# Layer input's gate in three fp32r products, the router's products inside mix_out, output weights in eight pieces, last units scaled by VectorE

## What is computed

```python
x = _layer_norm(DEEPNORM_ALPHA * x + m @ w_out, ln1_g, ln1_b)
# _moe: the router
scores = jax.nn.sigmoid((x @ w_router).astype(f32))        # 16 experts in 4 groups
biased = scores + router_bias
gsel   = argmax over groups of the sum of the two best
eidx   = the two best experts in that group
dest   = place of each (token, expert) pair in rows padded to 128 per expert
# layer input
ple_term = (ple @ w_ple) * jax.nn.sigmoid(x @ w_ple_gate)  # ple: 256 columns
x = _layer_norm(DEEPNORM_ALPHA * x + ffn + ple_term, ln2_g, ln2_b)
```

## Time and profile before

| | us |
|---|---|
| time before, median of 3 runs (2895.13 to 2896.97) | 2895.21 |
| the profiled execution | 2897.11 |
| its span, first to last instruction | 2895.0 |
| mix_out's first transfer to route's first | 2004.1 to 2157.7 |
| route's first transfer to the experts' first | 2157.7 to 2371.3 |
| experts' first transfer to the end | 2371.3 to 2895.0 |

### The profile page before, as it was taken

One profiled execution on the slowest core, in us unless ns is written; L12 is line 12 of the kernel. 1 busy time (PEld: TensorE's weight loads), 2 busy tenths in 40 slices (PEclk: granted clock), 3 DMA queues, 4 the chain that ended last, 5 costly groups with the idle time before them and its releaser, 6 DMA issues. The chain is left out here.

```text
span 2895.0 us, 41255 instructions
## 1 busy us (share of the span) xinstructions
PE 2533.8 (88%) x16099; PEld 2013.9 (70%) x16099; DVE 1236.3 (43%) x2155; ACT 1019.4 (35%) x1412; POOL 693.4 (24%) x537
## 2 busy tenths in 40 slices
PE   8989699969978996788868999997989979999991
PEld 7966456659958994777747888885447427877770
DVE  1042366645426654444431111110432107888876
ACT  1100277752232224455411111110001127777763
POOL 2231145432224324443301111110001430001002
PEclk9989699989989997999856999998987989999995
DMA  4363700021100004000040111112130029999986
GB/s 134 81 178 92 204 1 2 1 91 51 36 11 1 1 1 159 30 31 23 30 167 33 44 43 43 43 36 87 37 126 30 0 87 362 398 390 387 395 315 262
DMA packets 86455, 321.76 MB, mean 111 GB/s; under 512 B 14670, under 2 KB 35934, under 8 KB 66134
## 3 DMA queue, kind: packets, MB, share of 16 engines
q1 hardware_dynamic: 64966, 266.20, 25.4%
q10 hardware_dynamic: 12752, 28.14, 2.9%
q0 software_dynamic: 8608, 25.65, 2.5%
HBM read 281.40 MB, written 42.74 MB: 112 GB/s over the span
## 5 line engine op out<-in xcount | busy, mean ns | idle before, releaser
L2687 DVE TENSOR_TENSOR ex_low<-ex_raw,ex_high 128x2048 fp32r<-128x2048 f32 x138 | 308.7, 2287 | 141.3 <-ACT ex_high L2683 140.6
L2683 ACT ACTIVATE ex_high<-ex_raw 128x2048 fp32r<-128x2048 f32 x138 | 256.3, 1910 | 25.9 <-ACT o L2877 15.3
L172 PE MATMUL ps<-hx_high,mg_wg 128*128 128x344 f32 x576 | 191.6, 333 | 6.9 <-POOL mg_wg L2260 6.9
L174 PE MATMUL ps<-hx_low,mg_wg 128*128 128x344 f32 x576 | 185.1, 321 | 0.0
L173 PE MATMUL ps<-hx_high,mg_wg 128*128 128x344 f32 x576 | 184.8, 321 | 0.0
L1035 POOL TENSOR_SCALAR np_z<-np_z,np_sm 128x640 f32<-128x640 f32 (+12 forms) x128 | 125.4, 1003 | 231.1 <-DVE np_sm L1001 231.1
L2278 PE MATMUL ps<-o,hx_wb 128*128 128x344 f32 x576 | 170.4, 452 | 0.0
L2260 POOL TENSOR_TENSOR mg_wg<-hx_raw,mg_wg 128x1024 fp32r<-128x1024 f32 x24 | 56.4, 2352 | 429.4 <-ACT mg_wg L2288 429.4
L2698 PE MATMUL ps<-ex_high,ex_xh 128*128 128x512 f32 x368 | 150.3, 408 | 8.3 <-DVE ex_xl L2921 8.3
L2699 PE MATMUL ps<-ex_high,ex_xl 128*128 128x512 f32 x368 | 146.9, 399 | 0.0
L2700 PE MATMUL ps<-ex_low,ex_xh 128*128 128x512 f32 x368 | 146.6, 398 | 0.0
(11 more groups left out here) (556 smaller groups left out, 5967.7 us busy)
## 6 DMA issues: line engine op xcount, KB each, us to landing
ex_raw<-in_w_eg SPq DMA_DIRECT2D x46, 1024.0 KB, 7.2
ex_raw<-in_w_eu SPq DMA_DIRECT2D x46, 1024.0 KB, 9.4
ex_raw<-in_w_ed SPq DMA_DIRECT2D x46, 1024.0 KB, 9.8
hx_raw<-in_w_mg SPq DMA_DIRECT2D x24, 512.0 KB, 3.9
scratch_s_rows<-o ACTq DMA_DIRECT2D x23, 512.0 KB, 8.5
dnp_w<-in_w_dn SPq DMA_DIRECT2D x16, 512.0 KB, 3.4
hg_raw<-in_w_hg SPq DMA_DIRECT2D x16, 512.0 KB, 3.5
ns_pg<-in_cache SPq DMA_DIRECT2D x32, 192.0 KB, 2.8
```

The source lines that it names most:

```text
L172: pe.matmul(out, w[:, 0, k, :], x.high[:, k, tokens], start=first, stop=False)
L174: return pe.matmul(out, w[:, 0, k, :], x.low[:, k, tokens], start=False, stop=final)
L2683: act.activation(self.high[:, q], self.raw[:, q], ACT.Copy).then_inc(self.high_done[q], 1)
L2687: eng.tensor_tensor(self.low[:, q], self.raw[:, q], self.high[:, q], ALU.subtract).then_inc(self.low_done[q], 1)
```

## The change

- **mix_out**: w comes in eight transfers, one per contraction step, each with its own semaphore; the first half of tile 0's products waits for each in turn. The router's weights rw are loaded here. TensorE makes the router's products of tile t-2 after the products of tile t (the last two behind them), from an fp32 copy xf of one transposed tile, into PSUM bank 6. ScalarE copies a transposed tile twice: rounded to x1.high and exactly to xf. VectorE subtracts, into x1.low, at the end of each tile's normalization. The transposes of tile t wait for the low part of tile t-1.
- **route**: no router products; ScalarE takes the sigmoid at once. The gate's weights come in eight pieces of 512 KB through two raw buffers in `c.spare`; ScalarE rounds each to wh, POOL subtracts into wl, and a load waits until its buffer's low part is done. SP issues pieces 0 and 1 first, then the tables, pT and w_ple, then pieces 2 to 7. TensorE does units 0 and 1 ahead of the selection, unit 0 step by step as pieces are split; the others behind the counts. A gate step is three fp32r products. POOL scales units 0 to 9 and scatters after them; VectorE scales units 10 to 17 after its destinations.

```diff
@@ mix_out
-            sp.dma_start(w[:], dr["w_out"]).then_inc(s["w"], 16)
+            for k in range(KT):
+                sp.dma_start(w[:, k], dr["w_out"][:, k]).then_inc(s[f"w{k}"], 16)
+            sp.dma_start(rw[:], dr["w_router"]).then_inc(s["rw"], 16)
...
-            pe.wait_ge(s["w"], 16)
             def turn(t):
                 pe.wait_ge(s["y"], t + 1)
                 if t:
-                    pe.wait_ge(s["trc"], t)
+                    pe.wait_ge(s["low"], t)
...
+            def scores(t):
+                r = rows(t)
+                pe.wait_ge(s["xf"], t + 1)
+                if t == 0:
+                    pe.wait_ge(s["rw"], 16)
+                for k in range(KT):
+                    mm = pe.matmul(ps[0:r, 6, t * NE:(t + 1) * NE], xf[:, k, 0:r], rw[:, k, :], start=(k == 0), stop=(k == KT - 1))
+                mm.then_inc(s["scored"], 1)
...
                     for k in range(KT):
+                        if t == 0 and n == 0:
+                            pe.wait_ge(s[f"w{k}"], 16)
                         mm = pe.matmul(...)
                 mm.then_inc(s["mm"], 1)
+                if t >= 2:
+                    scores(t - 2)
                 if t:
                     turn(t - 1)
+            scores(NTT - 2)
             turn(NTT - 1)
+            scores(NTT - 1)
...
+            def low(t):          # VectorE; called for t-1 after y of tile t
+                dve.wait_ge(s["high"], t + 1)
+                dve.wait_ge(s["xf"], t + 1)
+                dve.tensor_tensor(in_x1(x1.low, t), turned(rows(t)), in_x1(x1.high, t), ALU.subtract).then_inc(s["low"], 1)
...
             def copy(t):         # ScalarE
                 act.wait_ge(s["tr"], t + 1)
+                act.activation(in_x1(x1.high, t), turned(r), ACT.Copy).then_inc(s["high"], 1)
+                if t:
+                    act.wait_ge(s["scored"], t)
+                act.activation(xf[:, :, 0:r].rearrange(...), turned(r), ACT.Copy).then_inc(s["xf"], 1)
@@ route
-    MID = 9
+    MID = 10
 sync
-            sp.dma_start(w[:], dr["w_router"]).then_inc(s["in"], 16)
+            ple.load(sp, range(0, 2))
             ... rb, tri, blk, tok as before ...
-            ple.load(sp)
+            ple.others(sp)
             sp.wait_ge(s["zero"], 1)
             sp.dma_start(dr["s_row"]..., zero[:]).then_inc(s["cleared"], 16)
+            ple.load(sp, range(2, KT))
 gpsimd
-            ple.gpsimd(pool, range(0, MID))
+            ple.take_low(pool)
+            ple.scaled(pool, range(0, MID))
             ... scatter as before ...
-            ple.gpsimd(pool, range(MID, ple.UNITS))
 tensor
-            ... router's products ...
-            ple.tensor(pe, range(0, 4))
+            pe.wait_ge(s["sig"], 1)
+            ple.tensor(pe, range(0, 2))
+            pe.wait_ge(s["in"], 64)
             pe.wait_ge(s["sel"], 1)
             ... rank and count products as before ...
-            ple.tensor(pe, range(4, ple.UNITS))
+            ple.tensor(pe, range(2, ple.UNITS))
 scalar
             ... two sigmoids, now of bank 6 ...
+            ple.take_high(act)
             ple.scalar(act)
 vector
             dve.tensor_copy(rt.dest[:], df[:]).then_inc(s["dest"], 1)
+            ple.scaled(dve, range(MID, ple.UNITS))
@@ LayerInput
+    def load(self, sp, ks):
+        for k in ks:
+            if k >= 2:
+                sp.wait_ge(self.s["low"], k - 1)
+            sp.dma_start(self.raw[:, k % 2], self.c.dram["w_ple_gate"][:, k]).then_inc(self.s[f"raw{k % 2}"], 16)
+    def take_high(self, act):
+        for k in range(KT):
+            act.wait_ge(self.s[f"raw{k % 2}"], 16 * (k // 2) + 16)
+            act.activation(self.wh[:, k], self.raw[:, k % 2], ACT.Copy).then_inc(self.s["high"], 1)
+    def take_low(self, pool):
+        for k in range(KT):
+            pool.wait_ge(self.s["high"], k + 1)
+            pool.tensor_tensor(self.wl[:, k], self.raw[:, k % 2], self.wh[:, k], ALU.subtract).then_inc(self.s["low"], 1)
...
             for k in range(KT):
-                pe.matmul(ps[0:r, q, :], self.x1T[:, k, tk], self.wg[:, k, cols], start=(k == 0), stop=(k == KT - 1))
+                if u == 0:
+                    pe.wait_ge(s["low"], k + 1)
+                out = ps[0:r, q, :]
+                pe.matmul(out, x1.high[:, k, tk], self.wh[:, k, cols], start=(k == 0), stop=False)
+                pe.matmul(out, x1.high[:, k, tk], self.wl[:, k, cols], start=False, stop=False)
+                pe.matmul(out, x1.low[:, k, tk], self.wh[:, k, cols], start=False, stop=(k == KT - 1))
```

More of the change, by code:

```diff
@@ L2340, in root, with mix_out @@
     act.activation(st[0:r, 14:15], st[0:r, 13:14], ACT.Sqrt, bias=eps[0:r]).then_inc(given, 1)
-def mix_out(c, mT, y, x1T):
+def mix_out(c, mT, y, x1):
     nc, ps, dr = c.nc, c.ps, c.dram
@@ L2352, in mix_out @@
         st = sb("st", [P, 16])
+        xf = sb("xf", [P, KT, BLK])
+        rw = sb("rw", [P, KT, NE])
         block = ctx.enter_context(nc.Block())
+        in_x1 = lambda part, t: part[:, :, t * BLK:t * BLK + rows(t)].rearrange("p (a b) t -> p a b t", a=2)
+        turned = lambda r: ps[:, 4:6, :].rearrange("p a (b t) -> p a b t", b=4)[:, :, :, 0:r]
         @block.sync
         def _(sp):
-            sp.dma_start(w[:], dr["w_out"]).then_inc(s["w"], 16)
+            for k in range(KT):
+                sp.dma_start(w[:, k], dr["w_out"][:, k]).then_inc(s[f"w{k}"], 16)
+            sp.dma_start(rw[:], dr["w_router"]).then_inc(s["rw"], 16)
             for k in range(2):
@@ L2408, in _ @@
                 dve.tensor_tensor(yy, yy, gb[0:r, 1], ALU.add).then_inc(s["y"], 1)
+                if t:
+                    low(t - 1)
+            low(NTT - 1)
         @block.scalar
@@ L2422, in _, with route @@
             copy(NTT - 1)
-def route(c, x1T, y, rt):
+def route(c, x1, y, rt):
     nc, ps, dr = c.nc, c.ps, c.dram
@@ L2592, in _, with __init__ @@
             dve.tensor_copy(rt.dest[:], df[:]).then_inc(s["dest"], 1)
+            ple.scaled(dve, range(MID, ple.UNITS))
 class LayerInput:
     UNITS = 2 * NTT
-    def __init__(self, c, x1T, y, sb):
-        self.c, self.x1T, self.y, self.s = c, x1T, y, Semaphores(c, "pl")
-        self.wg = sb("wg", [P, KT, D])
+    def __init__(self, c, x1, y, sb):
+        self.c, self.x1, self.y, self.s = c, x1, y, Semaphores(c, "pl")
+        self.wh, self.wl = sb("wh", [P, KT, D], FR), sb("wl", [P, KT, D], FR)
+        self.raw = c.spare.rearrange("p (j d) -> p j d", j=2)
         self.wp = sb("wp", [P, 2, D])
@@ L2605, in __init__ @@
         self.sg = sb("sg", [P, 2, 512])
-        self.pp = sb("pp", [P, 2, 512])
+        self.pp = c.rest.rearrange("p (j d) -> p j d", j=2)
     def unit(self, u):
@@ L2628, in tensor @@
             for k in range(KT):
[L2629 removed]
+                if u == 0:
[4 more added lines that the diff above has]
+                pe.matmul(out, x1.low[:, k, tk], self.wh[:, k, cols], start=False, stop=(k == KT - 1))
+            if u == 0:
+                pe.wait_ge(s["in"], 32)
             for k in range(2):
@@ L2644, in scalar, with scaled @@
             act.activation(self.sg[0:r, j], ps[0:r, q, :], ACT.Sigmoid).then_inc(s["read"], 1)
-    def gpsimd(self, pool, units):
+    def scaled(self, eng, units):
         s = self.s
@@ L2650, in gpsimd @@
             yv = self.y(t)[0:r, cols]
[L2651 to L2654, removed]
+            eng.wait_ge(s["read"], u + 1)
+            if u:
+                eng.wait_ge(s["used"], u)
+            eng.tensor_tensor(self.sg[0:r, j], self.sg[0:r, j], self.pp[0:r, j], ALU.mult).then_inc(s["scaled"], 1)
+            eng.wait_ge(s["scaled"], u + 1)
+            eng.tensor_tensor(yv, yv, self.sg[0:r, j], ALU.add).then_inc(s["used"], 1)
 class Pieces:
@@ L3100, in layer @@
         c.retire()
[L3101 to L3104, removed]
+    with ExitStack() as ctx:
+        x1 = Tokens(c, "x1", lambda n, sh, dt: ctx.enter_context(nc.sbuf_tensor(f"x1_{n}", sh, dt, side="right")))
+        with m_ctx:
+            mix_out(c, mT, y, x1)
+        route(c, x1, y, rt)
     experts(c, rt)
```

30 lines of the change are left out of this document (12 added, 18 removed).

## The result

The changed kernel takes 2877.21 us, median of 4 runs (2874.70 to 2879.15), against 2895.17 (2894.27 to 2896.97): a ratio of 0.9937, 95% interval 0.9919 to 0.9954. That is 18.0 us less; 23.6 less was predicted. A second comparison, with 13 runs of before, gave 2875.40 against 2897.32, 21.9 less (0.9923, 0.9905 to 0.9941).

The account below looks back on a forecast made before the run. TensorE's chain from the landing of the output weights to the last unit was taken as the bound. Terms -8.3 + 10.7 + 2.0 - 6.2 - 20.3 - 0.3 - 1.2 = -23.6 us gave 2871.6, range 2863 to 2885.

Parts of the forecast that it names:

- pieces: Start of mix_out: output weights in eight transfers let tile 0 end earlier, -8.3 us.
- scores of six tiles: In mix_out: router products of tiles 0 to 5 lie ahead of the last tile's end, 1.78 us each, +10.7 us.
- tail: End of mix_out, from tile 8's products to route's start: last scores and low parts lengthen it, +2.0 us (0 to 4).
- head: Start of route to the end of units 0 and 1: scores gone, weight splits added, 44.0 instead of 50.2 us, -6.2.
- sixteen units and restart: Route, behind the rank products: fp32r units of 7.32 us give -20.3, a cheaper restart at low clock -0.3.
- end: End of route: VectorE's last two operations take some 0.65 us each in place of POOL's, -1.2 us.
- the splits are the bound: Rival in route's head: longer loads or splits put the last split at 38 us into route; total 2878, 15%.
- Selection: In route's head: VectorE's router selection ends at about 35 us, before TensorE needs it at 44, costing nothing.
- The rival's mechanism: Rival in route's head: POOL's work holds up VectorE's selection, which ends at 50 instead of 44 us; total 2878, 7%.
- both rivals on the price of a product: Gate units: three fp32r products cost one fp32 product (total 2894, 4%), or each costs 0.214 us (2863.5, 2%).
- VectorE's share of the scaling: Late route: POOL scatters after unit 9, through at 147 us while TensorE runs until 180, hidden.
- Clock in mix_out: Rival: the clock falls in narrow work between mix_out tiles, costing 34 us; total 2906, 5%. The forecast had it hold.

Follow-up runs that it names:

- ring3: The change with three raw buffers instead of two and gate pieces 0 to 2 loaded during mix_out; ratio 0.9906 against the kernel before.
- pair: The change with units 0 and 1 made side by side, piece by piece, still two raw buffers; ratio 0.9908 against the kernel before.
- ring3_pair: The change with three raw buffers, pieces 0 to 2 loaded in mix_out, and units 0 and 1 side by side; ratio 0.9893 against the kernel before.
- two: The change without the gate's third product, low by high; units 5.42 us apart, ratio 0.9798 against the kernel before.
- poolall: The change with POOL scaling units 10 to 17 too, after its scatter, instead of VectorE; ratio 0.9939 against the kernel before.
- sums: ring3_pair4 with VectorE adding up the selection, so rank and count products need 19 products instead of 81; 2843.49 us against 2897.85 for the kernel before.
- scores2: The change with the router's 8 products of each tile made twice in mix_out; ratio 0.9992 against the kernel before.
- ring3_pair4: ring3_pair with units 2 and 3 also made ahead of the selection; ratio 0.9864 against the kernel before.

## Why the prediction was right, and where it was off

The direction, the bound (TensorE's chain) and the range held; 2871.6 was 5.6 low. In the profiled executions: 1.5 of it lies in the stretch, 5.1 in the experts, and the program reached mix_out 0.95 earlier. Term by term in the stretch:

| term | predicted | measured |
|---|---|---|
| pieces | -8.3 | -8.0 |
| scores of six tiles | +10.7 | +10.5 (2037.39 to 2150.27 is 112.9; before 102.4) |
| tail | +2.0 | +1.3 (2150.27 to 2160.60 is 10.3; before 9.0) |
| head | -6.2 | -2.9 (47.3; before 50.2) |
| rank products | 0 | +0.8 (16.9; before 16.1) |
| sixteen units and restart | -20.6 | -21.4 (118.7; before 140.1) |
| end | -1.2 | -2.4 (4.8 behind the last product; before 7.2) |
| sum | -23.6 | -22.1 |

- **Head.** The mechanism was right (`ring3`, `pair`), its size was the mis-sized term. Pieces 2 and 3, queued behind 2.1 MB, landed at 13.2 and 14.4 us instead of 11.7 and 13.1; piece 5 came 5.0 us after its buffer was free, beside piece 4 on its way, where 3.6 was assumed. That makes 2.6 of the 3.3; the rest is the low clock behind the splits, in the end of unit 0 and the first product of unit 1, which took some 2.8 of the 12.6 us from the last low part to the rank products, where 2.2 was allowed. The rival "the splits are the bound", with 38 for the last low part, had the right kind of error: 34.7 lies nearly half way.
- **Selection.** Predicted at about 35 and hidden; its last operation came at 31.6, hidden. The rival's mechanism showed when the head got shorter (`ring3_pair`). VectorE operations of 0.17 us took 2.24 and 2.33 beside a subtraction of 2.34. The Trainium skill ("SBUF — State Buffer", Who interferes with whom) calls it an exclusive lock of a port pair that the two engines share; these rows agree.
- **Units.** 7.30 for 7.32; both rivals on the price of a product fall with that and with `two`. The restart gained 0.9 instead of 0.3: unit 2 lost 1.7 us where the first unit behind the rank products had lost 2.7.
- **End.** The operations themselves gained 1.2, as said. Another 1.2 came from a place the sum did not have: behind POOL as the last engine the next stage's first load came 2.75 us later (2368.58 to 2371.33), behind VectorE 1.57.
- **VectorE's share of the scaling.** "Hidden with 30 us to spare" was right for the change as a whole, but the term was costed as if it stood alone. `poolall` shows that with faster units POOL's slack is used up; without the move 4.2 us of TensorE's time would have been lost.
- **Clock in mix_out.** It held, and 5% was perhaps low: the argument from 4.0 us of rank products at 1.00 was thin, since in `sums` the clock fell after 2.7 us of them, and `scores2` lost it in three tiles.
- **Luck in the sum.** That the stretch came out within 1.5 us is partly luck: by the table, the pieces, the head and the rank products fell short by 4.4 us together, and the scores, the tail, the units and the end made up 2.9.
- **Not priced, not tested.** No run undoes the move of the router's products alone. Its price is read from the traces: 10.5 and 1.3 us in mix_out, for 27.9 us at the low clock that route no longer has. But up to the last low part, 34.7 us into route, TensorE was busy for only 11.5, so by estimate most of the old products would have fitted into its waiting. The selection, which needs the scores, would then start some 27 us later (it started 33.5 us into route before, 6.3 now), and TensorE would need more units to make ahead of the rank products. Whether that is faster is open.
- **The time itself.** The range of 2863 to 2885 was for the sum. The experts' stage, which varies by 9 us from trace to trace, was not in it, and took up most of the miss of the profiled execution.

## What to carry to other kernels

A faster inner product pays only where its operands are there: here the split of weights took back 15 of 20 us, and a third buffer with early loads gave 10.8 of them back. Parts of a change are not additive: the move to VectorE was forecast at 1.2 us, and without it the faster units would have lost 7. Compare stages rather than totals when an untouched stage varies by more than the effect: the stretch repeated within 0.1 us while the gain in total time moved by 4.

## What was not expected of the hardware

- The granted clock fell at different points of the narrow work with 16 columns: 2.7 us (`sums`), 3.4 (the change), 5.2 (`ring3_pair4`) and 5.8 us (`ring3`) after its start, each time behind products at full clock.
- It rose amid the head of `pair` (0.97 from 2186 to 2203) and `ring3_pair` (1.00 from 2175 to 2191), in which TensorE still waited for the splits between steps, and stayed at 0.50 in the head of the change (2168 to 2195), which had half the work in each step.
- The experts' stage, which loads its weights in pieces of 1 MB, took between 462.7 and 472.0 us with the same code, over 14 traces.
